# Normalising the projection's input in the background, and the low-rank products in three rounded passes

## The reference

```
h = rmsnorm(x) * gain                    # x: 264 tokens x 1024
proj = h @ w_in                          # 1024 x 6440: r, k, v, three low-rank inputs, short conv, SSM
xs = proj + (prev - proj) * mu           # token shift, for the RWKV columns
w = w0 + tanh(w_lr) @ w2                 # 64 x 1024
a = sigmoid(a0 + a_lr @ a2)              # 64 x 1024
g = sigmoid(g_lr) @ g2                   # 160 x 1024
k = k * (1 + (a - 1) * k_a)
y_sc = rmsnorm(b_gate * conv3(c_gate * xt))
```

## Time and profile before

| | |
|---|---|
| time, median of 3 runs | 1662.56 us (1658.15 to 1662.92) |
| the profiled execution, its own time | 1660.52 us |
| its span, first to last instruction | 1658.5 us |
| mean granted TensorE clock | 0.986 of full |
| TensorE busy | 1550.0 us, 93% |
| VectorE busy | 1145.6 us, 69% |
| ScalarE busy | 860.9 us, 52% |
| GpSimd busy | 264.0 us, 16% |
| front stage's tiles, layer 1 | about 218 to 427 us |

### The profile page before, as it was taken

One profiled execution on the slowest core, in us unless ns is written; L12 is line 12 of the kernel. 1 busy time (PEld: TensorE's weight loads), 2 busy tenths in 40 slices (PEclk: granted clock), 3 DMA queues, 4 the chain that ended last, 5 costly groups with the idle time before them and its releaser, 6 DMA issues. The chain is left out here.

```text
span 1658.5 us, 41230 instructions
## 1 busy us (share of the span) xinstructions
PE 1550.0 (93%) x17275; PEld 1471.9 (89%) x17275; DVE 1145.6 (69%) x1832; ACT 860.9 (52%) x1521; POOL 264.0 (16%) x259
## 2 busy tenths in 40 slices
PE   7999999989799899999999999998997989899997
PEld 6999999977688789999999999998775878899997
DVE  6565578795798667665575656978768977676654
ACT  5444465767444555444354444657673445554443
POOL 0000003001455531000000000030014554300000
PEclk9999999999899999999999999999998999999999
DMA  7555557471244445555454655654703453465552
GB/s 232 178 168 176 161 157 211 131 210 52 64 127 119 138 150 171 196 174 187 149 186 153 203 166 175 194 157 131 213 1 104 126 166 111 130 199 181 187 176 71
DMA packets 280649, 256.26 MB, mean 155 GB/s; under 512 B 48054, under 2 KB 268700, under 8 KB 280450
## 3 DMA queue, kind: packets, MB, share of 16 engines
q1 hardware_dynamic: 276698, 252.05, 49.3%
q10 hardware_dynamic: 3768, 1.59, 0.4%
HBM read 242.22 MB, written 11.38 MB: 153 GB/s over the span
## 5 line engine op out<-in xcount | busy, mean ns | idle before, releaser
L209 ACT ACTIVATE front_hi<-front_raw 128x1024 fp32r<-128x1024 f32 (+2 forms) x230 | 238.5, 1039 | 257.2 <-PE ps L234 249.7
L216 DVE TENSOR_TENSOR front_lo<-front_raw,front_hi 128x1024 fp32r<-128x1024 f32 (+1 forms) x210 | 252.2, 1201 | 112.5 <-ACT front_hi L209 111.7
L209 ACT ACTIVATE out_hi<-out_raw 128x1024 fp32r<-128x1024 f32 (+1 forms) x168 | 173.2, 1038 | 216.1 <-PE ps L234 202.5
L216 DVE TENSOR_TENSOR out_lo<-out_raw,out_hi 128x1024 fp32r<-128x1024 f32 (+1 forms) x148 | 183.3, 1239 | 109.9 <-ACT out_hi L209 109.3
L232 PE MATMUL ps<-front_h_hi,front_hi 128*128 128x264 f32 (+1 forms) x816 | 241.2, 296 | 8.6 <-DVE front_lo L216 6.7
L234 PE MATMUL ps<-front_h_hi,front_lo 128*128 128x264 f32 (+1 forms) x816 | 233.0, 286 | 0.0
L233 PE MATMUL ps<-front_h_lo,front_hi 128*128 128x264 f32 (+1 forms) x816 | 232.8, 285 | 0.0
L232 PE MATMUL ps<-ffn_h_hi,out_hi 128*128 128x264 f32 x704 | 200.4, 285 | 0.1
L233 PE MATMUL ps<-ffn_h_lo,out_hi 128*128 128x264 f32 x704 | 199.6, 284 | 0.0
L234 PE MATMUL ps<-ffn_h_hi,out_lo 128*128 128x264 f32 x704 | 199.6, 283 | 0.0
L232 PE MATMUL ps<-in_h_hi,front_hi 128*128 128x264 f32 x688 | 197.3, 287 | 0.0
(11 more groups left out here) (410 smaller groups left out, 3861.2 us busy)
## 6 DMA issues: line engine op xcount, KB each, us to landing
front_raw<-in_w_in SPq DMA_DIRECT2D x50, 1024.0 KB, 5.4
out_raw<-in_ffn_w_in SPq DMA_DIRECT2D x44, 1024.0 KB, 5.2
front_raw<-in_ffn_w_in SPq DMA_DIRECT2D x40, 1024.0 KB, 5.3
back_sample_rows<-row_scratch SPq DMA_DIRECT2D x160, 128.0 KB, 3.1
out_raw<-in_w_out SPq DMA_DIRECT2D x16, 1024.0 KB, 5.8
front_raw<-in_ffn_w_out SPq DMA_DIRECT2D x16, 896.0 KB, 5.0
out_raw<-in_ffn_w_out SPq DMA_DIRECT2D x16, 896.0 KB, 4.9
front_raw<-in_ffn_w_out SPq DMA_DIRECT2D x8, 1024.0 KB, 5.4
```

Of the source, the lines that this page charges most:

```text
L209: act.activation(self.hi[n % self.RING][:, 0:k, 0:w], self._raw(n), ACT.Copy).then_inc(self.hi_ready, 1)
L216: eng.tensor_tensor(self.lo[n % self.RING][:, 0:k, 0:w], self._raw(n), self.hi[n % self.RING][:, 0:k, 0:w].bitcast(F32), ALU.subtract).the ...
```

## The change

Tiles 19 to 50 now use a normalised input: while tiles 8 to 18 run, VectorE multiplies x by gain and rs (`normed(k)`), ScalarE rounds it (`normed_hi`), VectorE takes the rest (`normed_lo`). Tiles 0 to 18 use the old form from another buffer. Late r, k, v tiles need no eviction: ScalarE reads the bank twice and VectorE's `mix_shifted` shifts straight from it; c and b tiles are multiplied in place. The b tiles move behind k. All low parts from tile 12 on are VectorE's. State decays are interleaved with the weighings (slots 25 to 30); short conv 2 and 3 move to slots 31 and 32; the rows for the new conv states are turned in three slots, 34 to 36, one bank; the short conv's mean moves to slot 37, the SSM's to 39, the key norms to 40 to 43, the bonus sums to 45, 47, 49, 50. The Ln group stands in slot 45, the Exp group in 46.

The low-rank weights are rounded by ScalarE in three chunks (`lora_hi`), GpSimd takes the low parts (`lora_lo`), and TensorE's `lora(p)` makes ten rounded matmuls of a block in place of four unrounded ones. The last 32 rows of g2 are loaded three times, so that their three passes are one product over 96 rows. The factor of k, `key_factor(p)`, moves from ScalarE to GpSimd.

```diff
         for kind, c0, first, count in (("xbc", X0, 0, 8), ("rwkv", 24 * P, 24, 2), ("z", Z0, 0, 4), ("x", SC0 + 1024, 0, 4),
-                                       ("c", SC0 + 512, 0, 4), ("b", SC0, 0, 4), ("rwkv", 8 * P, 8, 8), ("rwkv", 0, 0, 8),
...
-        H = len(tiles)
+        H, NORMED = len(tiles), 19
...
                                                                     *range(base + 4, base + 14, 2), *range(base + 26, base + 43, 2),
-                                                                    *range(base + 48, base + H, 2)})
+                                                                    *range(base + 12, base + H, 2)})
...
+        LORA = ((0, 3, at("w2_a2_hi0", 58880, [P, 3 * P], F32R), at("g2_hi0", 60416, [P, 3 * P], F32R), over_v("g2_stack0", 16, 3 * P)),
+                (3, 6, at("w2_a2_hi1", 51968, [P, 3 * P], F32R), over_v("g2_hi1", 18, 3 * P), over_v("g2_stack1", 20, 3 * P)),
...
+        lr_hi, lr_lo = over_v("lora_in_hi", 22, 2 * N), over_v("lora_in_lo", 24, 2 * N)
+        lr_stack = st.sb("lora_in_stack", [96, N], F32R)
...
-        norm2 = Norm(st, env, "mix", lambda k: env.col("norm_mix", k), A, h_hi, h_lo, rs, xa, ctmp[:, 0])
+        norm2 = Norm(st, env, "mix", lambda k: env.col("norm_mix", k), A, env.in_hi, env.in_lo, rs, xa, ctmp[:, 0])
...
+                    for i in range(3):
+                        sp.dma_start(g2b[32 * i:32 * i + 32], d["rwkv_g2"][layer][P:160]).then_inc(s("lora_in"), 16)
...
+                def lora_lo(i):
...
+                    pool.tensor_tensor(wa2_lo[:, c], wa2[:, c], wa_hi[:].bitcast(F32), ALU.subtract).then_inc(s("lora_lo"), 1)
+                    pool.tensor_tensor(g2_lo[:, c], g2[:, c], g_hi[:].bitcast(F32), ALU.subtract).then_inc(s("lora_lo"), 1)
...
+                    pool.tensor_tensor(stack[64:96], g2b[64:96, c], stack[64:96].bitcast(F32), ALU.subtract).then_inc(s("lora_lo"), 1)
+                    pool.wait_ge(s("lora_lo"), 3 * i + 3)
+
+                def key_factor(p):
...
-                    act.wait_ge(s("lora_read"), 3 * p + 2)
-                    act.activation(mix.bonus[:, p], mix.nb[:, p], ACT.Identity, scale=env.col("rwkv_k_a", p),
-                                   bias=env.oka[:, p:p + 1]).then_inc(s("fac_done"), 1)
...
+                def lora_hi(i):
...
+                    for hi, raw in ((wa_hi[:], wa2[:, c]), (g_hi[:], g2[:, c]), (stack[0:96], g2b[:, c])):
+                        act.activation(hi, raw, ACT.Copy).then_inc(s("lora_hi"), 1)
+
+                def normed_hi(k):
+                    act.wait_ge(s("normed"), k + 1)
+                    act.activation(h_hi[:, k], ctmp[:, k % 2], ACT.Copy).then_inc(s("normed_hi"), 1)
...
+                        if slot == 11:
+                            normed_hi(0)
...
+                    yield 12
+                    normed_hi(1)
                     yield 13
+                    normed_hi(2)
                     act.wait_ge(s("btok_ps"), 1)
                     act.activation(btok[:].rearrange("p c g n -> p (c g n)"), ps[:, A, :], ACT.Copy).then_inc(s("btok_done"), 1)
                     yield 14
+                    normed_hi(3)
...
+                        if h in (0, 2):
+                            normed_hi(4 + h)
+                            normed_hi(5 + h)
...
+                    act.wait_ge(s("lr_done"), 3)
+                    act.activation(lr_hi[:], mix.xs[:, 24:26].rearrange("p m t -> p (m t)"), ACT.Copy).then_inc(s("lr_hi"), 1)
+                    for i in (0, 64):
+                        act.activation(lr_stack[i:i + 32], mix.xs[0:32, 26], ACT.Copy).then_inc(s("lr_hi"), 1)
...
+                    for slot, m in ((25, 0), (26, 1), (27, None), (28, 2), (29, None), (30, 3), (32, None), (34, None)):
+                        yield slot
+                        if m is not None:
+                            decay(m)
+                        if slot in (27, 29, 32, 34):
+                            weigh_outer({27: 0, 29: 1, 32: 2, 34: 3}[slot])
...
+                    yield 35
+                    new_rows(0)
+                    yield 36
+                    act.wait_ge(s("lora_in"), 96)
+                    act.wait_ge(s("new_in"), 7)
+                    lora_hi(0)
+                    new_rows(1)
+                    act.wait_ge(evicted, 35)
+                    act.activation(sc_squares[:], acc, ACT.Square).then_inc(s("sc_sq"), 1)
                     yield 37
+                    new_rows(2)
                     act.wait_ge(s("y_gated"), 1)
...
+                    act.wait_ge(s("smp"), 4)
+                    lora_hi(1)
                     for p, slot in enumerate((40, 41, 42, 43, 44, 45, 48, 49)):
-                        yield slot
-                        if p == 5:
+                        if p == 2:
+                            yield slot
+                            act.wait_ge(s("rows_stored"), 64)
+                            lora_hi(2)
+                        if p == 6:
+                            yield 45
...
                             act.activation(nrm[:], nrm[:], ACT.Ln, scale=LN_SCALE).then_inc(s("norm_ln"), 1)
...
+                            yield 46
...
                             act.activation(nrm[:], nrm[:], ACT.Exp, scale=-0.5, bias=lnb[:, 0:1]).then_inc(s("norm_inv"), 1)
...
+                        yield slot
                         gates(p)
...
+                    if kind == "rwkv" and n >= NORMED:
+                        act.wait_ge(ws.used, base + n + 1)
+                        bank = ps[:, n % 3, 0:N]
+                        act.activation(mix.xs[:, m], bank, ACT.Copy, scale=env.omu[:, m:m + 1]).then_inc(kept, 1)
+                        act.activation(last[:, m], bank[:, T - 1:T + NS], ACT.Copy).then_inc(last_in, 1)
...
+                    if kind == "c":
+                        dve.wait_ge(evicted, n)
+                        dve.tensor_tensor(u[:, m, 2:2 + N], u[:, m, 2:2 + N], bank, ALU.mult).then_inc(evicted, 1)
+                        return
...
+                    if kind == "b":
+                        dve.wait_ge(s("smp_sc"), 5)
+                        dve.wait_ge(s("uconv"), 3 * (m + 1))
+                        dve.tensor_tensor(acc[:, m], acc[:, m], bank, ALU.mult).then_inc(evicted, 1)
+                        return
...
+                def mix_shifted(n, m):
...
+                    dve.scalar_tensor_tensor(out=mix.xs[:, m, 1:T], in0=bank[:, 0:T - 1], scalar=env.col("rwkv_mu", m),
+                                             in1=mix.xs[:, m, 1:T], op0=ALU.mult, op1=ALU.add).then_inc(evicted, 1)
+
+                def normed(k):
+                    if k >= 2:
+                        dve.wait_ge(s("normed_lo"), k - 1)
+                    dve.scalar_tensor_tensor(out=ctmp[:, k % 2], in0=env.x[:, k], scalar=env.col("norm_mix", k), in1=rs[:],
+                                             op0=ALU.mult, op1=ALU.mult).then_inc(s("normed"), 1)
+
+                def normed_lo(k):
+                    dve.wait_ge(s("normed_hi"), k + 1)
+                    dve.tensor_tensor(h_lo[:, k], ctmp[:, k % 2], h_hi[:, k].bitcast(F32), ALU.subtract).then_inc(s("normed_lo"), 1)
...
+                    yield 12
+                    normed_lo(0)
+                    normed(2)
+                    yield 13
+                    normed_lo(1)
+                    normed(3)
                     for j in range(4):
                         yield 14 + 2 * j
+                        if j < 2:
+                            for t in (2 + 2 * j, 3 + 2 * j):
+                                normed_lo(t)
+                                normed(t + 2)
+                        if j == 2:
+                            normed_lo(6)
+                            normed_lo(7)
...
+                    short_conv(0)
+                    yield 27
+                    short_conv(1)
...
+                    yield 31
+                    short_conv(2)
+                    yield 32
+                    short_conv(3)
+                    dve.wait_ge(s("smp_sc"), 5)
...
+                        if slot == 48:
+                            normed_keys(0)
+                            minus_b(0)
+                        if slot in (46, 48, 50, 51):
+                            for p in {46: (0, 1), 48: (2, 3), 50: (4, 5), 51: (6, 7)}[slot]:
...
+                    if late:
+                        mix_shifted(n, m)
...
+                def lora(p):
...
+                    pe.wait_ge(s("lora_lo"), 3 * (i + 1))
+                    gate = ps[:, EB, 0:N]
+                    for n, (w, x) in enumerate(((wa_hi[:, own], lr_hi), (wa_hi[:, own], lr_lo), (wa2_lo[:, c], lr_hi))):
+                        for h, bank in enumerate((A, DB)):
+                            mm = pe.matmul(ps[:, bank, 0:N], w[half[h]], x[half[h], 0:N], start=n == 0, stop=n == 2)
...
+                    pe.matmul(gate, g_hi[:, own], lr_hi[:, N:2 * N], start=True, stop=False)
+                    pe.matmul(gate, g_hi[:, own], lr_lo[:, N:2 * N], start=False, stop=False)
```

(26 more changed lines are left out.)

205 lines of the change are left out of this document (114 added, 91 removed).

## The result

The changed kernel takes 1680.91 us (median of 3 runs, 1678.9 to 1689.8), against 1662.56 before: a ratio of 1.0133, 95% interval 1.0085 to 1.0181 (the two medians alone would give 1.0110). It is slower, by 5 us more than the 1676 forecast. Its profiled execution took 1678.9 us, 18.4 more than the one before; its span is 1677.1, 18.6 more.

The account below looks back on a forecast made before the run. Front stage limited in turn by VectorE, TensorE, VectorE, TensorE (TensorE 93% busy overall). 5.4 + 2.1 - 0.4 - 0.5 = 6.6 us a layer, 13.2 in two, gave 1673.7 profiled; median 2.0 higher, 1676 us; range 1651 to 1688.

Parts of the forecast that it names:

- Low-rank block: Rounded low-rank products take 1.0 us a column block instead of 1.92, saving 7.4 us a layer over eight blocks.
- Slots 10 to 18: Normalising in the background delays copies and segments that TensorE awaits: a loss of 5.4 us a layer.
- The wait for b_tok: Slot 13: ScalarE's b_tok copy queues behind normed_hi(2); TensorE idles 4.0 us, its row matmuls 3.3 us later.
- The segments: Slots 14 and 16: normed operations precede the segments TensorE awaits, costing 1.1 and 0.6 us.
- the clock: Slots 10 to 18: after 4 us idle TensorE's clock may halve; half of 1.6, 0.8 us, counted.
- Slots 19 to 39: Longer waits in slots 32 (3.5) and 35 (4.7), partly caught up: 0.8 us later, 2.1 with moved key norms (1.3).
- Slots 40 to 50: Products save 6.4 us, new waits for gates, key norms and r_k lose 6.0: net -0.4 us a layer.
- Tail: From the last tile to the front stage's end, one shift shorter: -0.5 us a layer.
- The products win: Rival: b_tok and turned rows are ready, so the products' saving mostly remains: 1648 to 1652 us, chance 0.20.
- The clock falls more often: Rival: waits in slots 13, 32, 35, 40, 47 bring three more falls of 1.6 us a layer: 1685, chance 0.15.
- They cancel: Rival: slot 13's wait comes, slot 35's does not; time within 5 us of before, chance 0.14.
- The lock: GpSimd's stalls of 2.2 and 2.1 us on VectorE go; new work after slot 36 may add at most 3.

Follow-up runs that it names:

- e8: Changed kernel with unrounded matmuls, results overwritten, filling TensorE's idle times behind tiles 13, 15, 32, 35 and 47; 1679.30 us, ratio 1.0113.
- e3: Changed kernel with ScalarE's weigh_outer(3) moved from slot 34 to slot 35, behind the first turned rows' copy; 1682.67 us, ratio 1.0136.
- e10: e5 with TensorE's second row broadcast and weigh_outer(2) in slot 33, and new_rows(1) ahead of lora_hi(0); 1647.11 us, ratio 0.9923.
- e4: Changed kernel with Exp group in slot 47, bonus and r_k ahead of normed_keys(0) and minus_b(0), gates_zero ahead of lora_lo(1); 1665.27 us, ratio 1.0030.
- e6: Changed kernel with the low-rank products unrounded as before, four matmuls a block; 1682.75 us, ratio 1.0134.
- e9: e5 with the low-rank products unrounded as in the kernel before; 1656.98 us, ratio 0.9984.
- e5: Changed kernel with all the orders of e1 to e4 together; 1648.68 us, ratio 0.9937.
- e7: Kernel before the change, with low halves of tiles 14 and 16 made by VectorE in place of GpSimd; 1659.29 us, ratio 0.9998.
- e12: e10 with the low halves of tiles 36, 38 and 40 made by GpSimd in place of VectorE; 1654.37 us, ratio 0.9958.
- e2: e1 plus the segments ahead of VectorE's normed operations, and Exp ahead of normed_hi(4) to (7); 1667.93 us, ratio 1.0044.
- e1: Changed kernel with the b_tok copy put ahead of normed_hi(2) in ScalarE's slot 13; 1673.56 us, ratio 1.0080.

## Why the prediction was right, and where it was off

The direction, the mechanism (waits from order, not from work) and the places were right. The sum was 6.6 a layer against 9.9 measured; counted from tile 3, as in the table, it is 10.8 in the first layer and 11.7 in the second. That the forecast still came within 5 us of the median is in part luck: 4.0 us came off in stretches that the change hardly touches. By its steps, in layer 1 and from tile 3:

**Low-rank block.** Taken 1.0 us, measured 1.16: eight blocks save 6.1 a layer rather than 7.4, and near the upper bound of 1.20. The pairs do run side by side.

**Slots 10 to 18.** 5.4 forecast, 8.7 measured: 3.3 of the error of 4.2. The wait for b_tok was right (4.0 idle forecast, 3.7 measured; row matmuls 2.4 later on the clock of the trace, 3.3 against tile 3, as forecast). The segments cost 1.9 and 1.0 rather than 1.1 and 0.6. (The prediction's 3.3, 1.1 and 0.6 make 5.0, not 4.8, so its own sum is 0.2 short.) The term that was mis-sized most is the clock: 0.8 was counted for one possible fall at half chance; there were two falls, one behind the b_tok wait and one behind the wait of 2.0 for the segments, and they made tiles 14 and 16 1.3 and 1.5 us longer than before; e8 got 1.5 back from each. I had not given a wait of 2 us a fall, since the one of before stood behind 2.5; e8 shows that both are paid in full up to tile 32.

**Slots 19 to 39.** 2.1 forecast with the key norms that moved behind; measured 0.4 (tiles 19 to 40), which with the 1.3 of the forecast for the norms makes 1.7. The waits in slots 32 and 35 came (3.1 and 3.5 for 3.5 and 4.7) with clock falls, and were given back as the text said they would in part; e3 and e10 show that VectorE sets this stretch.

**Slots 40 to 50.** -0.4 forecast; measured 1.5, of which the 1.3 for the norms are already counted: 0.2. The parts came as laid out: gates 1.9 (2.5 forecast), key norms 1.2 (1.2), slot 47 2.5 (2.8), slot 49 0.9 (1.2; e4 made its tile 1.6 shorter). e6 confirms the sum, that the products' saving and these waits are about equal (unrounded products end layer 1's tiles 1.1 us earlier), and e4 and e9 confirm both sides of it. The clock fall behind slot 47, 1.3 by e8, was not in the sum.

**Tail.** -0.5 forecast, +0.3 measured; why is open.

**Rivals.** *The products win* lost for the reason given: VectorE was busy 38.9 of 40 us ahead of slot 13 and b_tok was late. Its time is about what e5 and e10 reach, 1648.7 and 1647.1, once the orders are changed. *The clock falls more often*: it did, six stretches in layer 1 for two, at the places named but slot 40, and behind slot 15, which it did not name. Its price of 1.6 holds for slots 13 and 15 (1.5 each) and nearly for 47 (1.3), but not for slot 32, which cost next to nothing; that of slot 35 no run isolates. That fits a time between the forecast and this rival. *They cancel* fails on slot 35, whose wait came; and e3 shows that taking it away alone would not have brought the time back.

**The lock.** The stalls of 2.2 and 2.1 us are gone, as forecast. By the Trainium skill, "SBUF — State Buffer", section "Who interferes with whom", an instruction of VectorE with two SBUF inputs and one of GpSimd that reads SBUF exclude each other. e7 and e12 agree (3.72 to 1.52; 1.25 alone, 3.31 beside a low half; a product with one input in PSUM unchanged at 1.29), and GpSimd pays as well: in e12 w_a_lo took 2.04 us beside kk_normed and 1.00 alone. GpSimd's new work behind slot 36 holds VectorE up as the prediction said it might: in the changed kernel a low half took 1.76 us for 1.22 and a small sum 0.79 for 0.23.

## What to carry to other kernels

Background work that costs an engine little in sum can cost much by where it stands: ask of each new instruction which release, ready already, is now queued behind it. A few lines of order turned +1.3% into -0.6%, and gains that measure nothing alone (rounded products, and in layer 1 the turned rows' order) appeared once the waits around them were gone, so an undo test of one part in a kernel full of waits says little about that part. Taking one wait off TensorE pays only where no other engine is full. A timeline without gaps tells that before the run; the busy share of a long window may hide it (VectorE 33.0 of 40 us in the changed kernel's third window, yet no gap for 17.7 us of it).

## What the runs showed of the hardware

The half clock came behind an idle TensorE of as little as 1.9 us (slot 40 in e2, e3 and e8), but not each time: the same wait of 1.9 in the changed kernel and in e1, and one of 2.4 in slot 36 of e10, left it at full. So a wait's length alone doesn't tell whether it costs 1.5 us more. Filling the idle time with matmuls of no use kept the clock at full in four of five places of layer 1, and the tiles behind at 3.0 rather than 4.5 us, so part of an idle time's price can be taken off without removing the wait; where 3.5 us of idle time remained (slot 35) it did not, and at the end of the stage the same filling won nothing. Unexpected too: low halves that only moved to an idle engine held up a small VectorE instruction by 0.8 us and through it a DMA queue by some 1 us, and the chain behind it, through ScalarE to TensorE, made the front stage 2.7 us longer.
